# The first attention's causal mask on VectorE instead of TensorE, and a new order of SP's transfers

## The reference, cut to what matters

```
c = cumsum(log_f, axis=1)
logits = (q_blk . kb) * scale + c[t] - c[s]          # per head, 128 queries x keys
logits = where(causal, logits, NEG)
probs = softmax(logits); out = probs @ vb
```

## Time and profile before

| | us |
|---|---|
| median of 3 runs | 1211.8 |
| range of the runs | 1211.11 to 1212.22 |
| the profiled execution's own time | 1212.24 |
| its span (first to last instruction) | 1210.4 |
| TensorE busy | 1192.0 |
| VectorE, ScalarE, GpSimd busy | 615.2, 551.2, 505.2 |
| mean granted TensorE clock | 0.999 of full speed |

### The profile page before, as it was taken

One profiled execution on the slowest core, in us unless ns is written; L12 is line 12 of the kernel. 1 busy time (PEld: TensorE's weight loads), 2 busy tenths in 40 slices (PEclk: granted clock), 3 DMA queues, 4 the chain that ended last, 5 costly groups with the idle time before them and its releaser, 6 DMA issues.

```text
span 1210.4 us, 15678 instructions
## 1 busy us (share of the span) xinstructions
PE 1192.0 (98%) x5842; PEld 992.5 (82%) x5842; DVE 615.2 (51%) x1461; ACT 551.2 (46%) x991; POOL 505.2 (42%) x279
## 2 busy tenths in 40 slices
PE   9999999999999999999999999999999999999998
PEld 8878778888888887799878788888888888888886
DVE  5789864774628264994963673944222231220002
ACT  6453574476522364545775785434322332221113
POOL 1428462345433424125252883443344434443441
PEclk9999999999999999999999999999999999999999
DMA  8204662302332523143123204222332333323221
GB/s 275 81 25 142 172 175 70 105 1 71 122 105 70 186 93 105 35 161 106 36 40 83 92 9 163 95 95 94 105 104 71 105 105 99 100 80 122 97 77 70
DMA packets 80475, 119.19 MB, mean 98 GB/s; under 512 B 16008, under 2 KB 42760, under 8 KB 80016
## 3 DMA queue, kind: packets, MB, share of 16 engines
q1 hardware_dynamic: 80400, 118.19, 30.0%
HBM read 107.67 MB, written 4.21 MB: 92 GB/s over the span
## 4 chain that ended last, share of the span: by engine, by line
PE 85%; DVE 5%; POOL 3%; ACT 3%; issue 2%; DMA 1%; SPq 1%; ACTq 0%; DVEq 0%; POOLq 0%
PE bank L1724 64%; PE bank L2045 9%; PE bank L1820 2%; PE bank L1788 2%; PE bank L1802 2%; PE bank L1866 2%; DVE sc L1424 2%; DVE m L1420 1%; PE bank L1764 1%; POOL w_lo L704 1%; POOL w_lo L687 1%; PE bank L1905 1%; ACT w_hi L807 0%; DMA w_raw<-in_w_in 0%; POOL mK L741 0%
## 5 line engine op out<-in xcount | busy, mean ns | idle before, releaser
L687 POOL TENSOR_TENSOR w_lo<-w_raw,w_hi 128x2048 fp32r<-128x2048 f32 (+4 forms) x80 | 357.8, 4473 | 580.0 <-ACT w_hi L775 522.6
L1724 PE MATMUL bank<-aH,w_hi 128*128 128x512 f32 x800 | 318.3, 398 | 1.9 <-DVE mqT L1599 1.1
L1724 PE MATMUL bank<-aH,w_lo 128*128 128x512 f32 x800 | 311.9, 390 | 0.0
L1724 PE MATMUL bank<-aL,w_hi 128*128 128x512 f32 x800 | 308.7, 390 | 0.0
L775 ACT ACTIVATE w_hi<-w_raw 128x2048 fp32r<-128x2048 f32 (+4 forms) x76 | 140.7, 1851 | 263.0 <-PE bank L1724 162.2
L1724 PEld LDWEIGHTS bank<-aL,w_hi 128*128 128x128 f32 x800 | 150.2, 188 | 32.3
L1724 PEld LDWEIGHTS bank<-aH,w_hi 128*128 128x128 f32 x800 | 150.7, 188 | 31.0 <-issue 3.2
L1724 PEld LDWEIGHTS bank<-aH,w_lo 128*128 128x128 f32 x800 | 150.6, 188 | 26.5 <-issue 0.2
L1173 DVE TENSOR_TENSOR fg<-bank,rB 128x512 f32<-128x512 f32 x22 | 15.1, 691 | 128.2 <-PE bank L1724 128.2
L1724 PE MATMUL bank<-w_hi,aH 128*128 128x512 f32 (+4 forms) x224 | 77.1, 344 | 1.0 <-ACT aH L1034 0.7
L1724 PE MATMUL bank<-w_lo,aH 128*128 128x512 f32 (+4 forms) x224 | 75.4, 337 | 0.0
(11 more groups left out here) (338 smaller groups left out, 2119.9 us busy)
## 6 DMA issues: line engine op xcount, KB each, us to landing
w_raw<-in_w_in SPq DMA_DIRECT2D x23, 1024.0 KB, 5.1
w_raw<-in_w_gate SPq DMA_DIRECT2D x22, 512.0 KB, 3.8
w_raw<-in_w_up SPq DMA_DIRECT2D x22, 512.0 KB, 4.8
w_raw<-in_w_down SPq DMA_DIRECT2D x11, 1024.0 KB, 4.9
w_raw<-in_w_merge SPq DMA_DIRECT2D x8, 1024.0 KB, 4.9
w_raw<-in_w_out SPq DMA_DIRECT2D x8, 1024.0 KB, 5.0
w_raw<-in_w_ple_gate SPq DMA_DIRECT2D x4, 1024.0 KB, 4.9
w_raw<-in_w_in SPq DMA_DIRECT2D x4, 512.0 KB, 7.4
```

Of the source, the lines that this page charges most:

```text
L687: pool.tensor_tensor(out=w_lo[:, c % 2, 0:n], in0=w_raw[:, c % 2, 0:n], in1=w_hi[:, c % 2, 0:n].bitcast(F32), op=ALU.subtract).then_inc(w_ ...
L1724: ins = pe.matmul(o, l, r, start=(kk == 0 and operand == ROUNDED and m == 0), stop=(kk == total - 1 and operand == REST), skip_group_check ...
```

## The change

- The table `cB` becomes two tables (one per head parity) of eight key blocks of 128 columns. SP loads the row of `c` into blocks 2 to 5 and its first block again into block 0, with two DMAs on the same semaphore.
- A new function `mask_bias(h)` on VectorE makes the masked blocks with three `tensor_tensor` adds per head, each of a table's blocks and the mask in SBUF: blocks 1 and 6 (in one instruction of 256 columns), 5, and 7. It waits for the head's row, and is called once before the attention's loop for head 0, and at the end of step 4h - 1 for head h = 1 to 7 (behind L1273, ahead of `split_pair` and the gate tiles).
- The bias of a unit is then a strided choice of blocks: 7; 0 and 1; 0, 3 and 6; 2 to 5. The first unit of a head waits for all its adds.
- The mask matmul, the two bfloat16 tiles, their casts and their semaphore go. A pad takes their place, so that the other tiles stay where they were.
- SP's order for heads 2 to 7: wait until TensorE has filled unit 4(h-1) - 1, stack the head, then wait until VectorE has evicted that unit, and load the row.

```diff
+MASKED_FROM = ((1, 7, 5, 3, 5, 1), (5, 6, 1, 5, 6, 1), (7, 8, 1, 2, 3, 1))
+BIAS_OF = ((7, 8, 1), (0, 2, 1), (0, 7, 3), (2, 6, 1))
...
-        ident16 = sb("ident16", [P, P], BF16)
-        diag16 = sb("diag16", [P, P], BF16)
+        sb("pad0", [P, P])
...
-        cB = place("cB", 98, [P, 2, S])
+        cB = [place(f"cB{i}", at, [P, 2 * NB, P]) for i, at in enumerate((98, 127))]
...
             def load_cum(h):
-                sp_.dma_start(cB[:, h % 2, :], cum_dram[h:h + 1, :].broadcast_to([P, S])).then_inc(cum_landed[h % 2], 16)
+                for first, n in ((2, NB), (0, 1)):
+                    row = cum_dram[h:h + 1, 0:n * P].broadcast_to([P, n * P])
+                    dst = cB[h % 2][:, first:first + n, :].rearrange("p c k -> p (c k)")
+                    sp_.dma_start(dst, row).then_inc(cum_landed[h % 2], 16)
...
                     for h in range(2, H):
+                        wait_filled(sp_, "fox.l", NB * (h - 1) - 1)
+                        stack_head(h)
                         wait_emptied(sp_, "fox.l", NB * (h - 1) - 1)
                         load_cum(h)
-                        stack_head(h)
...
+                    if name == "fox" and i < NU - 1 and i % NB == NB - 1:
+                        mask_bias(i // NB + 1)
                     if name == "fox" and i in PAIR_HI_AT:
                         split_pair(PAIR_HI_AT[i])
...
-            dve.tensor_copy(ident16[:], ident[:])
-            dve.tensor_copy(diag16[:], tab("causal")[:, 3 * P:4 * P]).then_inc(half_ready, 1)
...
+            def mask_bias(h):
+
+                dve.wait_ge(cum_landed[h % 2], 32 * (h // 2 + 1))
+                for o0, o1, o_step, i0, i1, i_step in MASKED_FROM:
+                    t, given = cB[h % 2][:, o0:o1:o_step, :], cB[h % 2][:, i0:i1:i_step, :]
+                    n = i1 - i0
+                    mask = tab("causal")[:, 3 * P:4 * P].rearrange("p (o k) -> p o k", o=1).broadcast_to([P, n, P])
+                    dve.tensor_tensor(out=t, in0=given, in1=mask, op=ALU.add).then_inc(bias_masked, 1)
+
             def fox_bias(h, b):
                 if b == 0:
-                    dve.wait_ge(cum_landed[h % 2], 16 * (h // 2 + 1))
-                return cB[:, h % 2, 0:(b + 1) * P]
+                    dve.wait_ge(bias_masked, 3 * h + 3)
+                first, end, step = BIAS_OF[b]
+                return cB[h % 2][:, first:end:step, :]
...
+            mask_bias(0)
             softmax("fox", sp, pT, fox_bias, low_rows, attB)
...
-                        if name == "fox":
-                            ins = pe.matmul(o[:, b * P:(b + 1) * P], ident16[:], diag16[:], start=False, stop=True,
-                                            skip_group_check=True)
```

More of the change, by code:

```diff
@@ L21 @@
 F32R = mybir.dt.float32r
-BF16 = mybir.dt.bfloat16
 ALU = mybir.AluOpType
@@ L441, in build @@
         gains_landed, cst_landed, small_landed, p_landed = sem("gains_landed"), sem("cst_landed"), sem("small_landed"), sem("p_landed")
-        ones_ready, half_ready = sem("ones_ready"), sem("half_ready")
+        ones_ready, bias_masked = sem("ones_ready"), sem("bias_masked")
         sq_ready, sum_ready, rt_ready = sem("sq_ready"), sem("sum_ready"), sem("rt_ready")
@@ L1250, in softmax @@
                         wait_filled(dve, name + ".l", i)
+                        shaped = [t[:, 0:n] if name != "fox" else t[:, 0:n].rearrange("p (c k) -> p c k", k=P)
+                                  for t in (sc_[:, i % RING, :], bank_of(name + ".l", i))]
                         empties(dve.tensor_tensor_reduce(
-                            out=sc_[:, i % RING, 0:n], in0=bank_of(name + ".l", i)[:, 0:n], in1=k_bias(h, b),
+                            out=shaped[0], in0=shaped[1], in1=k_bias(h, b),
                             scale=1.0, scalar=-3e38, op0=ALU.add, op1=ALU.max, accum_out=mx[:, i:i + 1]),
@@ L1878, in _ @@
             pe.wait_ge(cst_landed, 32)
-            pe.wait_ge(half_ready, 1)
             pe.wait_ge(split_lo, NB)
```

## The result

| | before | after |
|---|---|---|
| median of five runs each, us | 1211.8 | 1218.14 |
| range of the runs | 1211.11 to 1212.35 | 1216.13 to 1220.39 |
| profiled execution, its span | 1212.24, 1210.4 | 1220.39, 1218.5 |

The changed kernel is slower: ratio 1.0052, 95% interval [1.0042, 1.0063], about 6.3 us. The forecast was 2.9 us faster.

The account below looks back on a forecast made before the run. TensorE was taken as the bound; 1.02 + 0.24 - 0.5 + 1.7 - 0.07 - 0.9 + 1.35 + 0.12 = 2.96, taken as 2.9 us, gave 1209.3 profiled, 1208.9 median, range 1208.2 to 1210.0.

Parts of the forecast that it names:

- What bounds the kernel: Whole kernel: TensorE is busy 1192.0 of 1210.4 us; work on another engine is free until TensorE waits for it.
- Mask matmuls removed: First attention: each mask matmul removed saves 0.12 us a unit, 0.48 a head, but only where TensorE sets the pace.
- Table for head 0: Units 0 to 7: three adds take 0.8 us, unit 2 starts 0.34 later, then units 2 to 7 save 0.72.
- Stacking on TensorE's signal: Unit 8: the stacked key tile comes earlier, 0.35 us of wait is left, unit 8 starts about 137.4, 1.02 earlier.
- Lands 3.1 to 4.7 us after an issue, median 3.5 ... gives back 0.5: Units 8 to 10: cum's row lands about 139.0, VectorE evicts late, TensorE loses 0.5 us (none to 1.7).
- Steady heads: Units 10 to 23: 14 x 0.12 = 1.7 us gained, a head takes 6.43 us, VectorE's extra 0.8 a head is covered.
- the cover of 0.4 us for the row: Units 10 to 23: cum's row needs about 7.6 us from TensorE's signal to landing, VectorE comes after 8.0.
- Stop of head 6's adds by GpSimd, 0.9 us: Units 24 to 28: GpSimd subtractions stop two adds, about 1.9 us, 1.0 hidden, 0.9 paid (nothing to 2.9).
- The weight chunk: Units 29 to 31: weights' DMA issued 1.3 us earlier, 5.0 behind unit 23, transfer 5.25; TensorE gains 1.35 (0.7 to 1.5).
- The sum: Whole first attention: all terms give 2.96 us, taken as 2.9, and the gain stays to the end.
- covers are thin: Rival, chance 0.18: cum's row lands late or GpSimd scaling stops adds, 0.2 us for seven heads, gain 1.5, 1210.3.
- VectorE as the bound: Rival, chance 0.06: adds wait for GpSimd in every head, a table costs 2.3 us, about 3.7 slower, 1215.5.

Follow-up runs that it names:

- the one-row variant: The changed kernel with block 0 of the table written by an add on VectorE instead of a second DMA: 1214.15 us, ratio 1.0015.
- masks twice: The changed kernel with SP's old order, one row transfer per head and the 32 mask matmuls put back beside VectorE's adds: 1213.15 us, ratio 1.0009 to the kernel before.
- the changed kernel's second measurement: The changed kernel run again word for word, beside other variants: 1216.33 us, ratio 1.0038 to the kernel before.
- sixteen-partition variant: The changed kernel with the second row transfer of heads 2 to 7 going to 16 partitions, 8 KB for 64 KB: 1212.56 us, ratio 1.0004.

## Why the prediction was wrong, step by step

**What bounds the kernel: right.** The change counted by what it did to TensorE's queue.

**Mask matmuls removed, 0.12 us each: right.** Heads of 6.44 and, with no mask, 6.43 us.

**Table for head 0: small miss.** Forecast 0.34 late at unit 2. From unit 0 to unit 2 it took 1.27 us instead of 0.80, so 0.47; TensorE was 0.52 late already at unit 0. That part comes from earlier and varies with the kernel, from -0.27 to +0.55 here, with or without the change.

**Stacking on TensorE's signal: right, the close number partly by luck.** Unit 8 starts at 137.65 for 137.4, without the 0.35 us of wait that I had left. TensorE came there later than forecast, by its late start. And the first stacking transfer went out at 132.11, but the tile was there by 137.65, at most 5.54 us behind it, where I had priced 5.9.

**"Lands 3.1 to 4.7 us after an issue, median 3.5 ... gives back 0.5": the step that failed first.** From unit 8 to unit 10 TensorE took 4.31 us after and 2.41 before. With 0.24 for two masks this gives back 2.14, not 0.5, and more than the 1.7 I had as a bound. The landing times of a row that went out ahead of the stacking were used for two that go out behind it: the second goes out at 136.44 and not at 135.65 (0.5 of it is the late start), and takes 4.13 us. With one row transfer in this place (the one-row variant) the row took 4.20 us and landed at 140.00, so most of the lateness at unit 10 is the order's, and 0.6 us the second transfer's. Its 64 KB were priced at SP's issue time, and not by what they do to the transfers around them.

I also ended the account at unit 10. GpSimd's halves of the head pair wait for VectorE, so its scaling was late for the transposes before unit 12 (1.12 us), and `stack_head` of head 4 was late by its wait for these halves: its row then landed in 4.99 us at 154.84, VectorE waited 1.02 us, and TensorE lost 7.82 - 6.44 = 1.4 us from unit 16 to unit 20.

From unit 8 to unit 12 the changed kernel takes 9.37 us, with one row transfer 8.97, with that and the old order 6.40, and the new order with masks on TensorE 6.79: it takes the late row and the adds behind it together.

**Steady heads: right where nothing was late** (units 12 to 16 and 20 to 24, 6.44 us); the cover of 0.4 us for the row was not there for head 4. VectorE bears the adds: with masks twice the rhythm stays 6.90.

**Stop of head 6's adds by GpSimd, 0.9 us: too large.** The adds were stretched, as said, but to 1.26 us from 0.83. From unit 24 to 29 it took 7.72 us, against 7.35 before: 0.4 with the mask's share. The rows are the three adds, the first of them alone (its mean ns is the second figure behind the bar; elsewhere it is 426), and GpSimd's row beside it.

```profile
168.15 1.26 DVE L1461 TENSOR_TENSOR cB<-cB,cst 128x256 f32<-128x256 f32 x3
...
L1461 DVE TENSOR_TENSOR cB<-cB,cst 128x256 f32<-128x256 f32 x1 | 0.7, 654 | 0.0
...
167.22 1.29 POOL L710 TENSOR_TENSOR w_lo<-w_raw,w_hi 128x512 fp32r<-128x512 f32 x1 [0.96 <-ACT w_hi L813]
```

The first add began 0.93 us into the subtraction and ended 0.29 us behind its end. In the changed kernel's second measurement it took 771 ns and ended 0.29 us behind it again, and the add of the earlier trace rows 0.28. The Trainium skill, "SBUF — State Buffer", section "Who interferes with whom", states an exclusive lock on a shared port pair, and these rows agree. What failed is my count of two full stops: the adds met the last 0.36 us of one subtraction, not two whole ones.

**The weight chunk, "1.3 earlier. With the 5.25 us of transfer": failed the same way.** The issue came 4.9 us behind unit 23, as forecast. But the transfer took 9.51 us, not 5.25, with the two row transfers directly ahead of it. Units 29 to 31 took 7.88 us, not 3.84: 4.0 us off, the largest single miss, and then the 2.45 us of the clock, for which the sum had no term. The landing time that I took holds for what was ahead of it: six stacking transfers, and before them one row. With the new order and one row transfer it took 7.63 (mask matmuls) and 7.91 (adds), with the old order and two 8.00 and 7.27, with both 9.51 and 7.96. So each change of what precedes it makes it slow by itself. In the sixteen-partition variant, where the 256 KB row precedes it too, it took 5.82; why so little stays open.

**The sum.** By its terms unit 31 was to start 2.8 us earlier than before; it starts 5.3 later. Of these 8.1 us some 0.3 were there at unit 8, 1.6 came by unit 10, 1.4 by unit 12, 1.4 from unit 16 to 20 and 4.0 from unit 29 to 31; 0.6 came back at head 6, where the stop was smaller.

**The rivals.** The one for a late row ("covers are thin") had the mechanism in part and priced it at 0.2 us a head. VectorE as the bound did not happen. That the extra transfer is itself the cost was no rival at all: the text has it only as "one of them the extra first block".

By the experiments the loss in the median is: the second transfer 4 to 5 us (2.2 if the new order's pair starts from the second measurement); the new order about 2 with tables and one transfer (1212.09 to 1214.15), under 1 with the masks on TensorE, and 1 or nothing with both transfers (1217.13 to 1218.14 or 1216.33); adds against masks about even. The parts overlap, as the late chunk is in both.

## What to carry to other kernels

A small transfer is not priced by its issue: ask what stands behind it in the queue and how many pieces read the same bytes. Broadcasting one short DRAM row over 128 partitions slowed its neighbours; an add on the engine that already touches the table did the same work, and in mid-stage it cost nothing that shows (a head of 6.90 us with the masks kept). And when a late buffer is fed by work moved behind something else, follow its lateness past the first unit, through every engine that waits, to the next load.

## What the runs showed of the hardware

- 128 reads of the same 512 bytes (64 KB), six times in this stage, cost 4 us, while 128 reads of distinct rows of another tensor or 32 reads of 2 KB cost 1 us. The weight chunk behind them landed in 8.00, 5.14 and 5.33 us. In the changed kernel the DMA engines showed a busy share near 0.55 and 37 to 182 GB/s in the four microseconds behind the row transfers, and 347 in the next.
- TensorE stood 3.41 us, and the granted clock was 0.50 from there to 189 us, more than five microseconds into its work; after a wait of 3.10 us (old order, two transfers) it was 0.50 from 141 to 144 us. After waits of 1.77 and 1.80 us before unit 31 it stayed at 1.00.
- An add of 256 columns with both operands in SBUF that met a GpSimd subtraction ended 0.28 to 0.29 us behind the subtraction's end, in three cases: it took 654 and 771 ns where it met the rest of one of 1.29 us, and 4.82 us where it met one of 4.59 us nearly from its start. Without such a neighbour it took 426 ns.
